# Prompt attention with the values stationary, two heads side by side in the array, and the outputs kept feature-major

## The reference, cut to what matters

```python
def causal_attend(q, k, v, q_pos, k_pos):        # 8 heads, q and k 96 wide, v 64 wide
    s = jnp.einsum('...qhd,...khd->...hqk', q, k).astype(jnp.float32) * (QK_HEAD ** -0.5)
    mask = k_pos[None, :] <= q_pos[:, None]
    s = jnp.where(mask, s, jnp.finfo(jnp.float32).min)
    p = jax.nn.softmax(s, axis=-1).astype(v.dtype)
    return jnp.einsum('...hqk,...khd->...qhd', p, v)
...
    o = jnp.moveaxis(ob, 0, 1).reshape(b, s, N_HEADS * V_HEAD)
    return o @ w_out, ckv, kpe                   # w_out: 512 x 1024
```

## Time and profile before

| | |
|---|---|
| median of 3 runs | 3090.78 us (3090.75 to 3100.58) |
| span of the profiled execution, first to last instruction | 3083.6 us |
| PE busy, matmuls | 2933.5 us, 95% |
| DVE / ACT / POOL busy | 1911.6 / 968.2 / 371.0 us |
| prompt attention | 221.6 to 423.1 us of the span |
| output projection, its first transposes | from 987.7 us |

### The profile page before, as it was taken

The page is one execution under the profiler, slowest core; times in us unless marked ns, Lnnn a source line. Parts: engine busy times, 40 slices in busy tenths (PEclk is TensorE's granted clock), DMA queues, the critical chain, the costliest instruction groups (busy, mean ns, idle before and its releaser), DMA issues. The chain is left out here.

```text
span 3083.6 us, 54554 instructions
## 1 busy us (share of the span) xinstructions
PE 2933.5 (95%) x19232; PEld 2750.7 (89%) x19232; DVE 1911.6 (62%) x3783; ACT 968.2 (31%) x1739; POOL 371.0 (12%) x396
## 2 busy tenths in 40 slices
PE   8979889999998999999999988989989999999998
PEld 5646679998996899999999988989989999999998
DVE  3436667777775565666666666882246566666665
ACT  3433345555554322222222223222122222222221
POOL 1003300000000000000000018660000000000000
PEclk9988999999998999999999999999999999999999
DMA  3010013222221021111111114343111111111111
GB/s 111 28 23 1 35 46 81 73 75 70 75 74 47 27 62 42 41 48 47 48 41 54 35 45 138 87 110 119 49 58 49 42 44 51 41 47 46 49 35 69
DMA packets 262263, 174.37 MB, mean 57 GB/s; under 512 B 77977, under 2 KB 247658, under 8 KB 261818
## 3 DMA queue, kind: packets, MB, share of 16 engines
q1 hardware_dynamic: 261882, 171.85, 19.2%
q10 hardware_dynamic: 192, 0.13, 0.0%
HBM read 149.49 MB, written 22.29 MB: 56 GB/s over the span
## 5 line engine op out<-in xcount | busy, mean ns | idle before, releaser
L1641 PE MATMUL f_up<-h_hi,f_wu_hi 128*128 128x352 f32 x2112 | 460.3, 326 | 16.8 <-DVE h_lo L2155 15.1
L1641 PE MATMUL f_up<-h_hi,f_wu_lo 128*128 128x352 f32 x2112 | 457.6, 324 | 0.0
L1641 PE MATMUL f_up<-h_lo,f_wu_hi 128*128 128x352 f32 x2112 | 457.3, 325 | 0.0
L1641 PEld LDWEIGHTS f_up<-h_hi,f_wu_hi 128*128 128x128 f32 x2112 | 361.8, 190 | 18.0 <-issue 15.7
L1641 PEld LDWEIGHTS f_up<-h_hi,f_wu_lo 128*128 128x128 f32 x2112 | 365.0, 189 | 0.0
L1641 PEld LDWEIGHTS f_up<-h_lo,f_wu_hi 128*128 128x128 f32 x2112 | 361.0, 189 | 0.0
L2068 ACT ACTIVATE f_conv<-f_u_row,f_taps 128x1056 f32<-128x1056 f32 x88 | 111.8, 1271 | 754.1 <-DVE f_u_row L2185 754.1
L2254 DVE TENSOR_TENSOR resid<-resid,f_down 128x352 f32<-128x352 f32 x528 | 271.3, 518 | 111.6 <-PE f_down L2014 108.4
L2014 PE MATMUL f_down<-f_a_hi,f_wd_hi 128*128 (+1 forms) x960 | 318.7, 332 | 6.2 <-DVE resid L2254 5.9
L2014 PE MATMUL f_down<-f_a_hi,f_wd_lo 128*128 (+1 forms) x960 | 311.0, 324 | 0.0
L2014 PE MATMUL f_down<-f_a_lo,f_wd_hi 128*128 (+1 forms) x960 | 310.7, 324 | 0.0
(11 more groups left out here) (428 smaller groups left out, 5678.8 us busy)
## 6 DMA issues: line engine op xcount, KB each, us to landing
f_wu<-ffn_w_up SPq DMA_DIRECT2D x86, 512.0 KB, 3.8
ca_cache<-cache_ckv SPq DMA_DIRECT2D x256, 128.0 KB, 2.0
raw<-ffn_w_down SPq DMA_DIRECT2D x44, 512.0 KB, 4.4
raw<-ssm_w_out SPq DMA_DIRECT2D x16, 512.0 KB, 3.8
s_spill<-resid SPq DMA_DIRECT2D x8, 528.0 KB, 10.5
s_u<-sm_ut SPq DMA_DIRECT2D x8, 528.0 KB, 2.7
resid<-s_spill SPq DMA_DIRECT2D x8, 528.0 KB, 7.9
pj_xb<-x_prompt SPq DMA_DIRECT2D x8, 512.0 KB, 3.7
```

The costliest lines, as they stand in the source:

```text
L1641: mm = nc.tensor.matmul(out(c), w, x(c), start=(first and n == 0), stop=(last and n == 2))
```

## The change

Three things are changed in `attend_prompt`, and `add_attention` follows.

Units are now pairs of heads: head pair `hp`, block `i` in the order 7, 0, 6, 1, 5, 2, 4, 3, and the two heads `a` = 0, 1 of a block one after the other. All 64 units are written out, without loops. Blocks 4 to 7 have buffers of their own (`long_probs`, `long_probsT`), and so have blocks 0 to 3 (`short_...`). Turns stand two units behind the score, values four.

The values product has the values stationary (128 x 64) and the transposed probabilities moving (128 x 128). The first head of a pair goes to columns 0 to 63 of the array, the second to columns 64 to 127, so `out` is 128 features (of two heads) x 128 tokens. ACT copies it undivided to `oT` (features x tokens), a view of the memory of `o_all`.

The division comes once per head pair: DVE inverts 16 columns of masses, PE transposes them, ACT copies them to `inv_rows`, PE spreads them over the partitions by a product with the 0/1 matrix `pick` (made by POOL), and DVE multiplies `oT` by the result, 512 columns at a time. These stand two and four steps behind the pair's last unit, so inside the next pair.

The copies of queries on POOL are gone; its work for the S5 layer waits for units instead of heads. In `add_attention` only the new tokens' outputs are transposed; the prompt's are split from `oT`, 1024 columns at a time, in turn with the weights.

```diff
+    ORDER = (7, 0, 6, 1, 5, 2, 4, 3)
+    units = [(hp, i, a) for hp in range(H // 2) for i in ORDER for a in range(2)]
+    LAG_T, LAG_O = 2, 4
+    STEPS = NU + LAG_O - 1
...
+        def mass_step(hp):
+            return min(PER * hp + PER + 2, NU + 1)
+        def spread_step(hp):
+            return min(PER * hp + PER + 4, NU + 2)
...
+            eng = {"turn": ("dve", "act")[g % 2], "mass": "act", "spread": "dve"}[kind]
...
+            def turn_mass(g, hp):
+                pe.wait_ge(inverse_done, hp + 1)
+                nc.tensor.transpose(turn[0:PER, g % 2, 0, :], inv_mass[:, :], ident[:, :]).then_inc(turned, 1)
+
+            def spread(g, hp, half):
...
+                    mm = nc.tensor.matmul(turn[:, g % 2, y, :], pick[:, i * P:(i + 1) * P], inv_rows[:, :], start=True, stop=True)
...
+            def values(q):
...
+                if q >= 2:
+                    pe.wait_ge(o_kept, q - 1)
+                for a in range(2):
+                    wait_unit_kept(pe, 2 * q + a)
+                for j in range(i + 1):
+                    for a in range(2):
+                        h = 2 * hp + a
+                        mm = nc.tensor.matmul(out[a * VH:(a + 1) * VH, q % 2, 0:P], v_all[:, j, h * VH:(h + 1) * VH],
+                                              probsT_of(2 * q + a)[:, j, :], start=(j == 0), stop=(j == i), tile_position=(0, a * VH))
                 mm.then_inc(o_done, 1)
...
+            for n in range(STEPS):
+                if n < NU:
+                    score(n)
...
+                if n % 2 == 0 and n >= LAG_O:
+                    values((n - LAG_O) // 2)
+                for g in of_step[n]:
+                    if g >= 2:
+                        wait_kept(pe, g - 2)
+                    {"turn": turns, "mass": turn_mass, "spread": spread}[groups[g][0]](g, *groups[g][3])
...
         def _(act):
...
+            for n in range(STEPS):
+                if n < NU:
+                    exponentials(n)
+                if n == 7:
+                    prep.functions(act)
+                if n % 2 == 0 and n >= LAG_O:
+                    keep_out((n - LAG_O) // 2)
+                for g in of_step[n]:
+                    if groups[g][1] == "act":
+                        keep_turned(act, lambda o, i: nc.scalar.activation(o, i, ACT.Copy), g)
```

And in `add_attention`, on DVE (ACT has the same order):

```diff
             for k in range(KO):
                 dve.wait_ge(w_split, k + 1)
                 nc.vector.tensor_tensor(w_lo[:, k, :], w[:, k, :], w_hi[:, k, :], ALU.subtract).then_inc(w_low, 1)
...
+                dve.wait_ge(hi_done, k + 2)
+                nc.vector.tensor_tensor(oT_lo[:, k, 0:TP], oT[:, k, :], oT_hi[:, k, 0:TP], ALU.subtract).then_inc(lo_done, 1)
```

More of the change, by code:

```diff
@@ L926, in score @@
                     w = min(512, (i + 1) * P - c)
-                    mm = nc.tensor.matmul(scores[:, i % 2, c:c + w], q_h[:, half, i * P:(i + 1) * P],
+                    mm = nc.tensor.matmul(scores[:, n % 2, c:c + w], qT[:, h, i * P:(i + 1) * P],
                                           kT[:, h, c:c + w], start=True, stop=True)
                 mm.then_inc(s_done, 1)
[L931 to L941, removed]
@@ L943, in values, with turns @@
-            def values(h, i):
-                n = h * NQ + i
-                if isinstance(n, int) and n == 1:
-                    pe.wait_ge(qc_kept, KK)
[L947 to L954, removed]
+            def turns(g, n, j, m):
+                if j == 0:
+                    pe.wait_ge(p_done, n + 1)
+                for y in range(m):
+                    mm = nc.tensor.transpose(turn[:, g % 2, y, :], probs_of(n)[:, (j + y) * P:(j + y + 1) * P], ident[:, :])
+                mm.then_inc(turned, 1)
@@ L961, in cached_queries, with keep_turned @@
                 mm.then_inc(qc_done, 1)
[L963 to L971, removed]
-            prep.on_tensor(pe)
[L974 to L981, removed]
+            prep.on_tensor(pe)
+            for n in range(STEPS):
+                if n < NU:
+                    score(n)
+                if n < KK:
+                    cached_queries(n)
+                if n % 2 == 0 and n >= LAG_O:
[4 more added lines that the diff above has]
+                    {"turn": turns, "mass": turn_mass, "spread": spread}[groups[g][0]](g, *groups[g][3])
+        def keep_turned(eng, copy, g):
+            kind, _, _, what = groups[g]
+            eng.wait_ge(turned, g + 1)
+            if kind == "mass":
+                copy(inv_rows[:, :], turn[0:PER, g % 2, 0, :]).then_inc(kept[groups[g][1]], 1)
+                return
+            n, j, m = what
+            if j == 0 and n >= 4:
+                eng.wait_ge(o_done, n // 2 - 1)
+            copy(probsT_of(n)[:, j:j + m, :], turn[:, g % 2, 0:m, :]).then_inc(kept[groups[g][1]], 1)
         @block.vector
@@ L1049, in _, with exponentials @@
         @block.scalar
         def _(act):
[L1051 to L1052 removed]
+            def exponentials(n):
+                hp, i, a = units[n]
                 act.wait_ge(top_done, n + 1)
[L1054 to L1060 removed]
@@ L1087, in _, with keep_out @@
-            keep_probsT(H - 1, NQ - 1)
+                if n >= 4:
+                    act.wait_ge(turned, last_of_unit[n - 4] + 1)
+                col = PER * hp + 2 * i + a
+                nc.scalar.activation(probs_of(n)[:, 0:(i + 1) * P], scores[:, n % 2, 0:(i + 1) * P], ACT.Exp,
+                                     bias=top[:, n % 2:n % 2 + 1], scale=SCALE, accum_out=mass[:, col:col + 1]).then_inc(p_done, 1)
+            def keep_out(q):
+                hp, i, _ = units[2 * q]
+                act.wait_ge(o_done, q + 1)
+                nc.scalar.activation(oT[:, hp, i * P:(i + 1) * P], out[:, q % 2, 0:P], ACT.Copy).then_inc(o_kept, 1)
```

262 lines of the change are left out of this document (124 added, 138 removed).

## The result

The change made the kernel slower, by an amount just above what can be told from nothing. Runs of the kernel before taken beside those of the changed kernel have medians of 3094.3 and, in a second group, 3092.5 us. One of the first nine executions before took 4129.77 us and is left out of the ratio.

What follows compares the result with a forecast made beforehand. PE's work, then its waits for ACT's copies, bound the prompt attention; -16.5 (stage at full clock, including +3 for tile changes), +3 and +8.5 (clock), -2.5 (projection) gave -4.5: 3086 us, range 3066 to 3107.

Steps and rivals of the forecast that it cites:

- rival 2: Prompt attention: the clock, once fallen, stays low for long, over 10 us each; +28 in place of 11.5, 3102 us, chance 17%.
- The values pitch: Values product: both column halves work at once, 0.21 us a block pair, 31 us less PE work in the stage.
- The waits: PE idles ahead of short blocks' values: 3.2, 2.7, 2.3, 1.9 us behind ACT's copy; 3.6 less a pair behind DVE's.
- the walk: Prompt attention's new period step by step: 43 us a head pair with ACT's copies, 39.4 with DVE's, 165 for four.
- The output projection: Fewer transposes, split made from SBUF: -2.5 us, first sum near 12.5 us behind its stage's start.
- Rivals 1, 3 and 4: Clock holds: 28%, 3075 us; halves do not overlap: 5%, 3112 us; waits smaller than walked, no falls: 5%, 3060 us.
- rival 5: Values calls: each change between whole array and halves waits for a whole tail, 18 us in place of 3; 3101 us, 2%.
- point (2): Clock falls after PE's idle pieces in the prompt attention: five at 1.7 us each, +8.5 us, bounds 0 and 18.
- +3 at the start: Low clock at the prompt attention's start doubles PE's work there unless it rises sooner: +3 us, bounds 0 and 7.
- The tail: Behind the last score: transposes, mass, spread and two multiplications in series, about 9 us from the last period's end.
- -16.5: Prompt attention at full clock: its end moves from 423.1 to 406.6 us.
- the changes between whole array and halves: Entering and leaving column strips at 32 values calls: 0.05 to 0.15 us a change, 2 to 5 us, +3 in the sum.

Runs made afterwards that it cites:

- e7: Changed kernel with the values loops exchanged, all products of head a and then all of head b, so halves run in turn: 3122.9 us, ratio 1.0105.
- e5: The changed kernel again, unchanged, for a second profile: 3104.9 us, ratio 1.0039 to the kernel before.
- e2: Changed kernel with four unread products of 256 columns added ahead of the short blocks' values, filling PE's waits: 3097.1 us, ratio 1.0030.
- e6: Changed kernel with the engine that copies each group of transposes fixed by place instead of alternating: 3081.1 us, ratio 0.9967.
- e11: Changed kernel with values and copy-outs one pair of units later, run a second time: 3070.1 us, ratio 0.9934.
- e1: Changed kernel with values and copy-outs one pair of units later (6 steps behind the scores instead of 4): 3068.9 us, ratio 0.9928.
- e10: Kernel before with values and copy-outs one unit later (3 steps behind the scores instead of 2): 3069.0 us, ratio 0.9931.
- e9: Changed kernel with values one pair of units later and the column halves in turn instead of at once: 3079.7 us, ratio 0.9967.
- e4: The kernel before again, unchanged, for a second profile: 3098.9 us.

## Why the prediction was wrong

The forecast was -4.5 us, the result +12. The value lies in the range, on the other side of no change. The range reaches that far only because it took in rival 2.

**Right.** The values pitch: 32 passes in 1.97 us, 0.22 a block pair, and e7 shows what it would be otherwise. The waits: at rows 3, 0, 1 and 2 behind ACT's copy 3.1, 2.6, 2.2 and 1.7 us, behind DVE's 2.0, 1.6, 1.25 and 0.9, 3.8 us a pair less; the walk had 3.2 to 1.9, and 3.6 less. From 229 to 420 us e5 has 28 waits of over 0.2 us, 34.2 us in all, and with each goes the modelled tail that hides part of it, 0.28 - 0.11 = 0.17: 39 us together, where the walk had 2 x 12 + 2 x 8.4 = 40.8. The output projection: -2.9 for -2.5, its first sum 12.3 us behind the stage's start (1004.83 to 1017.13) for 12.5. Rivals 1, 3 and 4 did not happen; rival 5 neither, see below. The head pairs themselves took 47 to 53 us, outside the 39 to 46 that were to show the forecast.

**The step that failed is the clock's**, point (2) and what it left out. It had five falls at 1.7 us, +8.5, and +3 at the start. Measured in both profiles of the changed kernel: six falls of 3.4 to 10.2 us inside the stage, 30.7 and 27.3 us in all, hence 12 to 14 us at 0.44. The tail, which the sum ran at full clock, is at half clock in both:

```profile
429.80:439.70 9.90, 8.20 (x48) 6.81 (x44) 2.07 (x3) 1.42 (x4) 0.04 (x1) 0.50 0.00 0
```
```profile
423.80:433.40 9.60, 7.91 (x43) 6.77 (x42) 2.07 (x3) 1.42 (x4) 0.03 (x1) 0.50 0.00 0
```

That is 4 us more, of which the sum had nothing. The start cost 9 us in one profile and nothing in the other. Together the low clock cost 26 and 16 us of this stage, where the sum had 11.5. The sum also compared unlike things: its -16.5 is a stage at full clock against one that had 20.5 us at half clock, so 9 us of it are the low clock of the kernel before and not cheaper values. Clock against clock, the sum had +2.5 us and the profiles have +17 and +7. Taking off the half-clock time at 0.44 leaves 190.7 and 190.6 us, against 188.9 before (at 0.5 it is 187.1, 188.4 and 187.7). By this estimate the stage gains nothing at full clock, and the clock makes nearly all of its loss of 9 and 19 us. The 19 and 72 executions say the same without a profile. The Trainium skill ("TensorE: Matmul & The Clock Gate", Loop structure matters more than you think) has long waits between matmuls send the clock down; e2 and e6, with 10.4 and 5.1 us at half clock, agree, and e11, with short waits and 46.7 us, is not explained by it.

**The second error is the walk at full clock**: those 191 us stand against 184 forecast (197.9 - 16.5 + 3). The first three head pairs, from the first score of 7a to the fourth, took 156.4 and 146.3 us with 46.8 and 23.9 at half clock. At full clock that is 136 in both, and the sum has 135 for them, so the periods were right. What is missing stands in the last pair and the tail behind it, 55 us in both for 49; which part of them is not shown. One term is shown to be too small, the changes between whole array and halves, +3 in the sum. In e1, where no wait hides them (timeline):

```profile
271.39 0.39 PE L977 MATMUL pa_scores<-kT,qT 96*128 96x128 f32 x2
271.71 1.31 PE L1012 MATMUL pa_out<-pa_long_probsT,v_all 128*64 128x128 f32 x20
272.95 0.66 PE L985 MATMUL pa_turn<-ident,pa_long_probs 128*128 128x128 f32 x4
```

Two passes at 0.107 and 0.32 to the next start leave 0.10 for entering; 20 passes at 0.055 and 1.24 leave 0.14 for leaving; other calls of e1 agree to 0.01. 32 calls make 8 us, where the bounds were 2 and 5. In the changed kernel 25 of the 32 entries stand under a wait, so there it is 5 to 6 by this estimate. A whole tail each time (rival 5) would be 18. The drain of which the Trainium skill speaks ("TensorEngine Tiling (Array Packing)", Key Properties) is there, at a third to half of a tail.

Rival 2 gave nearly the right time, 3102 us, by a mechanism that did not occur: single falls lasted 3.4 to 10.2 us, not over 10; more of them, and the tail, made up the sum.

**What the argument missed altogether** is e10: as much as I credited to cheaper values, 16.5 us, could be had from PE's waits in the old order alone. I read them as what PE lacks and did not ask what they were worth by themselves: 18 us ahead of the values by PE's own list. The change took 31 us of PE work (by the pitches) from an engine that was waiting already, lengthened its waits (18 to 35 us) and so let its clock fall: shorter waits (e6) and filled ones (e2) both brought most of the clock back. The gain was given back there; once nothing waits (e1 against e9) the halves are worth 10 to 12 us of their 25, and the order, division and shape changes around them cost about as much, since e1 and e10 take the same time.

Open: why the clock of one and the same kernel falls in one execution and not in the next (e1, e11; e4), and whether filled waits pay.

## What to carry to other kernels

Before making an engine's work cheaper, look at what it waits for: moving the consumer one unit further behind its producer took a few lines and gave more than the restructuring, in the old order as in the new. A walk at full clock needs a second walk at the lower one: here the sparse tail and the waits of 2 to 3 us ahead of the values were where it fell most often, and e6 shows waits 8 us shorter bringing 22. When both sides of a sum do not stand at the same clock, take each to full clock first. Take two profiles of each kernel before a difference is put down to a stage: here one layer moved by 13.5 us between two executions of the same program. The mean granted clock of every execution costs nothing to read and showed more here than any single profile.

## What was not expected of the hardware

- Products into the same column half, each with other weights, go at 0.099 us a pass of 128 columns, a little under the 0.107 of full-width passes; in alternating halves 0.055.
- A microsecond at half clock cost 0.43 to 0.44 us in three comparisons of one kernel with itself, a little under half of it.
- Filler products on PE in waits: 15 us more of PE busy time than in e5, and the run is no longer (e2).
- The low clock at the start of this stage ended at 225 to 228 us in most profiles of the new order and only at 242 to 244 in two (the changed kernel's first, e11), the order being the same.
